# One norm for two behind the experts, scans for the states, a four-column-group compression and fillers in a two-block transformer on one core

## The reference

```python
def first_block(x, c, positions, ...):
    for l in range(2):
        sh1, sc1, g1, sh2, sc2, g2 = split(silu(c) @ w_ada[l] + b_ada[l])   # 6 x 1024
        h = rms_norm(x, g_norm_mix[l]) * (1 + sc1) + sh1
        aq, ak, av, iq, ik, iw, bq, bf, bi, bg, cuv = split(h @ w_in[l])
        a_out = dsa_mixer(...)     # rope, index scores, the 64 best keys of each token, softmax
        b_out = hgrn2_mixer(...)   # recurrence: state = decay * state + k^T v, in chunks
        c_out = gmlp_mixer(...)    # gelu, layer norm, a 128x128 triangular mixing
        x = x + g1 * (concat(a_out, b_out, c_out) @ w_out[l])
        h = rms_norm(x, g_norm_ffn[l]) * (1 + sc2) + sh2
        y = swiglu(h) if l == 0 else moe_swiglu(h)     # 8 experts, best 2 of each token
        x = x + g2 * y
    return rms_norm(x, g_final)

def second_block(x, positions, ...):
    for l in range(2):
        h = rms_norm_2(x, ln1_gain[l])
        proj = h @ w_in[l]
        # compress_blocks, for keys and for values:
        #   blk = tok[:, tok_idx] + pos_emb   (15 blocks of 32 tokens, 2 groups)
        #   gelu(blk @ w1) @ w2               (2048 -> 128 -> 64)
        x = x + concat(o_nsa, o_mla, o_ret) @ w_out[l]
        x = x + square(relu(rms_norm_2(x, ln2_gain[l]) @ w_up[l])) @ w_down[l]
    return rms_norm_2(x, final_gain)
```

## Time and profile before

| | us |
|---|---|
| timed runs, median of 3 | 2725.51 |
| profiled execution, its own time | 2719.74 |
| profiled execution, span in the trace | 2717.9 |
| TensorE busy in the span | 2531.5 (93%) |
| VectorE busy | 686.4 (25%) |
| ScalarE busy | 388.2 (14%) |
| GpSimd busy | 0.2 |
| mean clock granted to TensorE | 0.961 of 2.4 GHz |
| head, until the first projection | 0 to 50.75 |
| block 1, layer 0: mixers, then dense network | to 269, to 505 |
| block 1, layer 1: mixers, router, experts | to 726, to 745, 753.5 to 1748.3 |
| the two norms behind the experts | 1750 to 1771.19 |
| block 2, layers 0 and 1 | to 2236, to 2703.6 |
| last norm, turning, stores | to 2717.9 |

### The profile page before, as it was taken

One profiled execution on the slowest core, in us unless ns is written; L12 is line 12 of the kernel. 1 busy time (PEld: TensorE's weight loads), 2 busy tenths in 40 slices (PEclk: granted clock), 3 DMA queues, 4 the chain that ended last, 5 costly groups with the idle time before them and its releaser, 6 DMA issues.

```text
span 2717.9 us, 33588 instructions
## 1 busy us (share of the span) xinstructions
PE 2531.5 (93%) x14380; PEld 1972.9 (73%) x14381; DVE 686.4 (25%) x1944; ACT 388.2 (14%) x1002; POOL 0.2 (0%) x4
## 2 busy tenths in 40 slices
PE   6998999997799989998999999789899999989998
PEld 4666888765688658756875786476588888658887
DVE  2565543257400000000000000124431111443111
ACT  3221000121200000000000000223410002341001
POOL 0000000000000000000000000000000000000000
PEclk7998999999799999999999999989999998999999
DMA  9363686422267999799789979933234431323410
GB/s 340 116 235 114 221 305 242 142 94 93 93 225 280 367 393 350 284 394 394 293 334 395 381 281 365 360 104 108 94 124 155 155 123 46 123 80 140 151 66 16
DMA packets 269605, 582.81 MB, mean 214 GB/s; under 512 B 19078, under 2 KB 46350, under 8 KB 269456
## 3 DMA queue, kind: packets, MB, share of 16 engines
q1 hardware_dynamic: 268612, 579.51, 58.2%
q10 hardware_dynamic: 844, 1.12, 0.1%
HBM read 579.57 MB, written 1.05 MB: 214 GB/s over the span
## 4 chain that ended last, share of the span: by engine, by line
PE 85%; DMA 6%; DVE 5%; ACT 3%; issue 1%; SPq 0%; ACTq 0%; DVEq 0%
PE wrk L2024 15%; PE acc L1418 11%; PE acc L746 10%; PE wrk L2665 8%; PE acc L2060 7%; PE wrk L1401 6%; PE wrk L2037 5%; DMA ring<-in_moe_w_up_dram 5%; PE acc L749 3%; PE acc L2071 2%; PE acc L828 2%; PE wrk L874 1%; PE acc L2079 1%; PE wrk L712 1%; PE acc L820 1%; PE acc L2087 1%
## 5 line engine op out<-in xcount | busy, mean ns | idle before, releaser
L2024 PEld LDWEIGHTS wrk<-hT,ring 128*128 128x128 f32 x3584 | 410.2, 195 | 25.9 <-issue 14.9
L2024 PE MATMUL wrk<-hT,ring 128*128 128x128 f32 x3584 | 413.0, 278 | 15.8 <-DMA ring<-in_moe_w_up_dram 9.1
L1418 PE MATMUL acc<-scratch,ring 128*128 128x256 f32 x1376 | 300.4, 379 | 0.0
L746 PE MATMUL acc<-hT,ring 128*128 128x256 f32 (+2 forms) x1152 | 279.7, 401 | 13.6 <-ACT hT L706 12.9
L1418 PEld LDWEIGHTS acc<-scratch,ring 128*128 128x128 f32 x1376 | 261.1, 190 | 35.3
L746 PEld LDWEIGHTS acc<-hT,ring 128*128 128x128 f32 (+2 forms) x1152 | 220.6, 195 | 64.6 <-issue 21.5
L2665 PE MATMUL wrk<-hT,ring 128*128 128x256 f32 x1024 | 223.3, 379 | 0.0
L2665 PEld LDWEIGHTS wrk<-hT,ring 128*128 128x128 f32 x1024 | 194.6, 190 | 26.5
L2037 PE MATMUL wrk<-ring,hT 128*64 128x256 f32 x1792 | 200.4, 381 | 4.3 <-DMA ring<-in_moe_w_up_dram 2.9
L2060 PE MATMUL acc<-ring,scratch 128*128 128x512 f32 x448 | 196.5, 593 | 0.0
L2037 PEld LDWEIGHTS wrk<-ring,hT 128*64 128x64 f32 x1792 | 126.3, 137 | 72.7 <-issue 8.0
(11 more groups left out here) (339 smaller groups left out, 2130.4 us busy)
## 6 DMA issues: line engine op xcount, KB each, us to landing
ring<-in_moe_w_gate_dram SPq DMA_DIRECT2D x56, 2048.0 KB, 12.9
ring<-in_moe_w_up_dram SPq DMA_DIRECT2D x56, 2048.0 KB, 12.7
ring<-in_moe_w_down_dram SPq DMA_DIRECT2D x56, 2048.0 KB, 12.4
ring<-in_w_ada_dram SPq DMA_DIRECT2D x24, 2048.0 KB, 12.9
ring<-in_w_up_dram SPq DMA_DIRECT2D x16, 2048.0 KB, 8.6
ring<-in_w_down_dram SPq DMA_DIRECT2D x16, 2048.0 KB, 7.5
ring<-in_w_out_dram SPq DMA_DIRECT2D x8, 2048.0 KB, 7.8
ring<-in_w_in_dram SPq DMA_DIRECT2D x6, 2048.0 KB, 13.3
```

What stands on the lines that cost most here:

```text
L746: mm = pe.matmul(acc[p0:p0 + m, bank, 0:S], cols(k), hT[:, k, :], start=(k == 0), stop=(k == KD - 1))
L1418: mm = pe.matmul(accv[:, m, :], w[:, j, m * P:(m + 1) * P], F_ACT[:, 4 * (g % 2) + j, :], start=(g == 0 and j == 0 and m % 2 == 0), stop=( ...
L2024: mm = pe.matmul(wrk[:, j, lo:lo + P], w[:, k, j * P:(j + 1) * P], hT[:, k, 0:P], start=(k == 0), stop=(k == KD - 1))
```

## The change

These parts are changed together:

1. *Head.* Positions and constants are loaded first on ScalarE's queue; the 18 `vec_loads` go to GpSimd's queue. `tables_dve` comes first on VectorE, `tables_act` before all copies of parts; two buffers of parts instead of one; the lower bounds go behind the index. `vec_pe` stands behind the fourth product.
2. *Order in block 1.* New step tables; four banks (`bank1`) until the heads; the top-k (`topk_dve`) behind two of the ropes; the gmlp mixer earlier in the bands; a new order of the ring.
3. *States.* `picks_dve` makes tiles of 4 chunks, half as wide; `kv_pe` makes 8 products of 64 rows per pair of heads instead of 4 of 128; the states lie `[v, b]`; GpSimd spreads the decays; `states_dve` is two scans; chunk 0 is left out of `inter_pe`.
4. *Fillers.* `keep_busy_pe(pe, 14)` behind the sums of all norms but the first one.
5. *One norm for two* behind the experts: with s the mean of x^2 and q that of (g x)^2, the second scale is 1/sqrt(q + EPS*(s + EPS)).
6. *Norm of block 2, layer 1:* gain and scale in one VectorE operation per slice.
7. *Compression:* the blocks are the stationary operand, in four column groups, joined by two matmuls between `cq0` and `cq1`; value blocks on VectorE.
8. *End:* squares and gain beside the last residuals, the result turned without its scale, which is applied as it is copied out, one half by each of two engines; four stores.

```diff
@@ head
         def start_act(act):
+            for b, name in enumerate(("positions", "positions_2")):
+                r = g[name]
+                act.dma_start(pos[:, b, :], bass.AP(tensor=r.tensor, offset=r.offset, ap=[[0, P], [1, S]])).then_inc(rest_landed, 16)
+            act.dma_start(const[:, REST], g["consts"][:, REST]).then_inc(rest_landed, 16)
...
-            for place, src in vec_loads:
-                act.dma_start(place, src).then_inc(params_landed, 16)
...
+        def start_pool(pool):
+            pool.wait_ge(dve_done, at("dve", "rows cleared"))
+            for place, src in vec_loads:
+                pool.dma_start(place, src).then_inc(params_landed, 16)
@@ order tables
-        BEFORE_INDEX = ("p iq0", "p iq1", "p iw0", "p iw1", "p ik", "r iq0", "r iq1", "p aq0", "r ik", "p aq1")
-        AFTER_INDEX = ("p aq2", "p av0", "p av1", "p bf0", "r ak", "p bf1", "r aq0", "p bf2", "r aq1", "r aq2")
+        BEFORE_INDEX = ("p iq0", "p iq1", "p ik", "r iq0", "p iw0", "r iq1", "p iw1", "r ik", "p aq0", "r ak")
+        AFTER_INDEX = ("p aq1", "r aq0", "p aq2", "r aq1", "p av0", "p av1", "p bf0", "p bf1", "p bf2", "r aq2")
...
+        def bank1(n):
+
+            return n % 4 if n < FIRST_BESIDE else 2 + n % 2
@@ states
+        def wide_decays_pool(pool, l):
+
+            pool.wait_ge(dve_done, at("dve", "whole", l))
+            pool.wait_ge(act_done, at("act", "kdec", l))
+            for a in range(3):
+                pool.tensor_copy(r_wide[a], r_whole[:, a, :].unsqueeze(1).broadcast_to([P, SCAN, NB])).then_inc(pool_done, up("pool", "wide", l, a))
...
         def states_dve(dve, l, a):
 
-            dve.memset(r_state[a][:, 0, :], 0.0).then_inc(dve_done, up("dve"))
             dve.wait_ge(act_done, at("act", "kv", l, a))
-            for b in range(1, NB):
-                settle(dve, "dve", dve_done)
...
+            dve.wait_ge(pool_done, at("pool", "wide", l, a))
+            wide = r_wide[a].rearrange("p v b -> p (v b)")
+            for i in range(HD // SCAN):
+                part = r_state[a][:, SCAN * i:SCAN * (i + 1), :].rearrange("p v b -> p (v b)")
+                dve.tensor_tensor_scan(part, wide, part, 0.0, ALU.mult, ALU.add)\
+                   .then_inc(dve_done, up("dve", "states", l, a) if i == HD // SCAN - 1 else up("dve"))
@@ inter_pe
-                        mm = pe.matmul(accv[rows, 4 + a, b * C:(b + 1) * C], r_state[a][rows, b, :],
+                        mm = pe.matmul(accv[rows, 4 + a, b * C:(b + 1) * C], r_state[a][rows, :, b - 1],
@@ norms
+            if tag != ("mix", 0):
+                keep_busy_pe(pe, 14)
+
+        def keep_busy_pe(pe, n):
+
+            for _ in range(n):
+                pe.matmul(acc[:, 0, 0:S], ones, K("slot_ids"), start=True, stop=True)
...
+        def joint_norm_pe(pe):
+            for k in range(KD):
+                pe.wait_ge(act_done, at("act", "squares", JOINT, k))
+                for bank, squares in ((3, hT), (2, gained_squares)):
+                    mm = pe.matmul(wrk[:, bank, 0:S], ones, squares[:, k, :], start=(k == 0), stop=(k == KD - 1))
+                    if k == KD - 1:
+                        mm.then_inc(pe_done, up("pe", "sum of squares", bank))
+            keep_busy_pe(pe, 14)
@@ compression
+            for turn in range(4):
+                for a in range(2):
+                    for q in range(4):
+                        j = 4 * turn + q
+                        mm = pe.matmul(wrk[32 * q:32 * q + 32, a, 0:P], n_blk[:, a, j, :], w1[:, a, j, :], start=(turn == 0), stop=(turn == 3),
+                                       skip_group_check=True)
...
-                for j in range(16):
-                    mm = pe.matmul(wrk[:, 0, 32 * a:32 * a + 30], w1[:, a, j, :], n_blk[:, a, j, :], start=(j == 0), stop=(j == 15))
+                mm = pe.matmul(wrk[:, 3, 32 * a:32 * a + 30], n_part[:, a, :], K("fours"), start=True, stop=True)
@@ end
+            for k in range(KD):
+                pe.wait_ge(act_done, at("act", "end h", k))
+                for t in range(2):
+                    mm = pe.matmul(wrk[:, 2 + t, 0:1], end_squares[:, k, t * P:(t + 1) * P], ones[:, 0:1], start=(k == 0), stop=(k == KD - 1))
```

370 lines of the change are left out of this document (255 added, 115 removed).

## The result

The changed kernel takes 2659.86 us (median of 4 runs, 2657.66 to 2664.58), the kernel before 2725.12 beside it: a ratio of 0.976, 95% interval 0.974 to 0.978. It is faster by 65 us; 2646 had been forecast, with 2617 to 2675 as the range. The spans of the two profiled executions are 2717.9 and 2659.1, 58.9 apart.

The account below looks back on a forecast made before the run. TensorE's own work was taken as the bound, 85% of the span, so gains lie in its waits, costly work and low clock. Terms summed to -79 from 2719.7, giving 2640.7, or 2646 against the 2725.5 median; range 2617 to 2675.

Parts of the forecast that it names:

- rival A: Block 1: VectorE stays the bound, scans, finer picks and GpSimd copies give back the gains; 2666 us, chance 0.20.
- Head: Kernel start: angles no longer wait for VectorE's other work, first projection at 38.2 instead of 50.75; -12.5 us.
- Index and attention's start: Block 1: four banks before the index, -2 us; ropes ahead of the top-k, -3.5 in layer 1 and -1.5 in layer 0.
- Heads, bands, key-value products: Block 1: layer 0 gets work in pauses and the kv group shrinks in both layers; -5 and -1.5, together -6.5 us.
- States: Block 1's states, inter and output projection: scans replace dependent chains, TensorE sees about half of 10 us a layer; -8 us.
- Fillers: Behind norm sums: 14 matmuls take 6.3 us in place of a wait, partly repaid by the full clock; +2.8 us.
- One norm for two: Behind the experts: one set of sums and a filler replace two norms, first projection at 1765.3, clock up; -7 us.
- Compression: Block 2: column groups side by side, about 2.0 us plus join, less idle, full clock behind; -18 and -16.5, together -34.5.
- rival B: Block 2's compression: column groups do not overlap, 9.2 instead of 2.2 us a layer, no clock gained; 2666 us, chance 0.07.
- D: Head: vector loads on GpSimd's queue stall while VectorE computes tables, arriving 4.2 us late; 2650 us, chance 0.08.
- E: Head: vector loads hold the first projection, at 6 us a load +94; slower kernel at 2740 us, chance 0.02.
- C: Router, bands and behind the states: the clock stays up further than counted, about 10 us; 2636 us, chance 0.13.

Follow-up runs that it names:

- last-but-one run: Changed kernel plus split output projection, old order beside heads and bands, no filler at block 2's second layer, lower bounds beside the first head: 2636.28 us, ratio 0.967.

## Why the forecast was right, and where its steps failed

The sign, the size within 14 us of 65, and the range held. The point lies between the forecast (2646) and rival A (2666), nearer to A, and what put it there is in block 1. The four terms there (index, attention's start, bands with key-value products, states) were to give 21.5 us; they cost 7, although a filler's 1.8 us is in them. That is more than rival A took back. The time stays below A's only because compression and end gave 8 us more than forecast, so part of the hit is luck.

- **Head, right** (-12.1 for -12.5), by two errors that cancel: the tile came later than 31, the product behind it ran at the full clock. The forecast's own terms add up to 38.0, not 38.2. In the other runs with this head the first projection starts at 38.7 to 41.3, so that it is 38.6 in this one is luck too.
- **Index and attention's start, right in sum** (-9.8, of which 1.8 is the filler's, for -7). In layer 0 the lower bounds cost a wait of 4.33; the last-but-one run took it away.
- **Heads, bands, key-value products, wrong:** +7.5 for -6.5. The step that failed is that layer 0 has work to put into pauses and the key-value group shrinks. VectorE has as much to do as before. The group's own products did shrink, but its copies, priced nowhere in the forecast, doubled from 0.97 to 1.88, and the pauses came to 2.0 at the low clock. The old order gave back 3.3 us in these stages, the split output projection 10. The sign that was named for layer 1, bands to output projection shorter by 5 (by less than 2 for rival A), came out as A's: 67.4 us before, 67.9 after.
- **States, wrong:** +9.3 for -8. Three steps failed. One is "TensorE sees about half" of the 10 us: the last chain showed a wait of 0.87, not 5. The second is the strided weight, for which a price was named (a doubling, 5.5 us a layer): it did nearly double, 0.031 to 0.057. The terms as they are written, -5 and -1.7 a layer, make -6.7 and not the -3.8 and -4.3 of the sum, so some 3 us a layer were allowed for it without being said. The third is the clock, -1.7 a layer in the 20 records behind the reads: they became longer instead (+1.1 and +0.7), and so did the products ahead of the reads and the last ones of the output projection. The scan takes 1.17 us and not 0.7. The Trainium skill (DVE: opcode table, instruction layouts, handler registers and perf-mode slots, §6 Datapath and trigger behaviour) states half throughput for it, from which the forecast had estimated 1.1; the trace agrees (1.17 beside 0.68 for the two-input operation). It did not matter, since nothing waited for the scans.
- **Fillers, right in kind:** about even over all. The router's share was underrated, that of block 2's second layer rightly seen as a loss (1.6 forecast, 2.5 measured in the step).
- **One norm for two, right in kind, too large:** -3.8 and 1.8 of clock behind it, for -7. The sums start 2.56 us behind the last expert product instead of 1.34, and the first seven of the sixteen run at the low clock: 10.0 us, not 7.2. Why they start so late is open: the first squares were ready at 1743.4, the sums began at 1746.31. The doubled squares are not the reason, since the run with two norms has one square for each slice and the same 2.5 us.
- **Compression, larger than forecast:** the two rows of block 2 together are -44.2; with 1.8 booked to the norm's filler and 1.6 to the last filler (96 records of the first projections, 22.35 to 20.72 in layer 1) it is -40.8 for -34.5. The terms for the clock were too small: the forecast took the old 13.83 and 11.91 us as the price of the form, though most of it was measured at the low clock. The mechanism was in part right: overlap of column groups, on which rival B hung, gave 2.4 us of 11.9 in layer 0. No row shows the 0.144 us a record that the forecast took for products one behind the other; the run with the groups in turn has 0.068, so that without overlap a layer costs some 2.4 us more and not the 7 of rival B.
- **End, right:** -7.9 for -6.3. The 16 column sums took 3.63 and the turning ran faster than before (2.68 for 3.68).

Rival A named the right place and half of the reason: in layer 1's bands VectorE is the bound. The picks moved into the bands gave back 3.8 us. But scans and GpSimd's copies (1.94 for three) did not; layout did, through ScalarE's copies and the weight loads, and the clock behind pauses. Rivals B, D and E did not come; C did not, since the mean clock rose from 0.961 to 0.969 only.

## What to carry to other kernels

When a data layout is turned for one engine's sake, price it on every engine that touches the tile: here the scan's layout saved 7.3 us a layer on VectorE, of which TensorE had waited for 0.9, and it doubled the copies on ScalarE and the reads of the states on TensorE. Read first what the bounding engine waits for; how busy the other one is says nothing of it. And put real work into short pauses between dependent groups before any filler: moving 10 products a layer into two gaps of 2 us gave 10 us in two layers, while five fillers gave nothing together that is clear of the noise. When a stage is measured at the low clock, its time is not the price of its form: look at the clock before the gain is split.
